# Moving the filter spectra behind the projections, with one third of the conditioning weights left ahead of them

## The reference, cut to what matters

```python
ada = silu(c) @ w_ada + b_ada                      # c: 1024, w_ada: 1024 x 6144
sh1, sc1, g1, sh2, sc2, g2 = split(ada, 6)         # six vectors of 1024
u = x * (1 + sc1) + sh1                            # needs the first third of ada
proj = u @ w_in                                    # Hyena, attention and gate parts
# Hyena branch: implicit filters, long convolution through spectra
h = sin(f1_freq * (feats @ f1_w + f1_b))           # 1024 x 64
h = sin(f2_freq * (h @ f2_w + f2_b))               # 1024 x 64, "hidden"
h = (h @ f3_w).reshape(1024, 2, 2, 512) * decay    # taps, forward and backward, 2 orders
K = rfft(concat([fwd, 0, reversed bwd]))           # spectra, independent of x and c
z = x1 * long_conv(v, K[:, 0]); z = x2 * long_conv(z, K[:, 1])
# attention branch, gates, output projection:
x = LN(alpha * x + (1 + g1) * mix)                 # needs the second third of ada
x = LN(alpha * x + (1 + g2) * peer(x * (1 + sc2) + sh2))   # PEER, 128 x 128 experts, top 16
```

## Time and profile before

| | us |
|---|---|
| median of three runs | 4256.4 |
| the execution that was profiled | 4264.03 |
| its span, first to last instruction | 4262.2 |
| setup, to the next stage's first transfer | 39.4 |
| spectra, to the next stage's first transfer | 200.5 |
| attention projections | 231.3 |
| attention and other projections, to the long convolution | 520.1 |

### The profile page before, as it was taken

The page is one execution under the profiler, slowest core; times in us unless marked ns, Lnnn a source line. Parts: engine busy times, 40 slices in busy tenths (PEclk is TensorE's granted clock), DMA queues, the critical chain, the costliest instruction groups (busy, mean ns, idle before and its releaser), DMA issues. The chain is left out here.

```text
span 4262.2 us, 57381 instructions
## 1 busy us (share of the span) xinstructions
PE 3770.9 (88%) x19170; PEld 3277.4 (77%) x19170; DVE 2565.5 (60%) x5465; ACT 1396.8 (33%) x2897; POOL 1153.5 (27%) x797
## 2 busy tenths in 40 slices
PE   6889899998879798999989889896888988898896
PEld 3579788886657687999988879896677777777775
DVE  5563133224544413999988778785766666666667
ACT  1110122221123211233278888796211111111111
POOL 1132121112322021333343333332323232323330
PEclk9789999998989899999999999898999999999998
DMA  4741212215543222333379999999867677777773
GB/s 176 285 148 40 81 65 81 76 61 217 197 147 124 79 80 90 130 131 132 119 249 329 305 313 322 294 333 304 293 241 238 238 240 244 236 244 246 242 256 136
DMA packets 502745, 826.90 MB, mean 194 GB/s; under 512 B 289175, under 2 KB 309911, under 8 KB 496440
## 3 DMA queue, kind: packets, MB, share of 16 engines
q1 hardware_dynamic: 111848, 370.03, 24.8%
q0 software_dynamic: 84096, 318.80, 21.2%
q10 hardware_dynamic: 306576, 135.28, 12.7%
HBM read 679.31 MB, written 144.70 MB: 193 GB/s over the span
## 5 line engine op out<-in xcount | busy, mean ns | idle before, releaser
L79 PE MATMUL va_fps<-va_vt_h,va_c_h 128*128 128x512 f32 x1536 | 631.1, 411 | 184.6 <-DVE va_vt_l L2204 176.0
L80 PE MATMUL va_fps<-va_vt_l,va_c_h 128*128 128x512 f32 x1536 | 621.9, 405 | 0.0
L81 PE MATMUL va_fps<-va_vt_h,va_c_l 128*128 128x512 f32 x1536 | 621.0, 404 | 0.0
L2082 POOL DMA_INDIRECT va_rows<-in_vtab,k_pick x256 | 377.3, 1474 | 850.4 <-DVE k_big L2228 748.0
L79 PEld LDWEIGHTS va_fps<-va_vt_h,va_c_h 128*128 128x128 f32 x1536 | 305.6, 199 | 262.9 <-issue 164.6
L1916 ACT ACTIVATE ga_first<-ga_first,ga_gs 128x128 f16<-128x128 f16 x1536 | 470.2, 398 | 85.0 <-DVE ga_first L1975 84.8
L79 PE MATMUL ga_aps<-k_u_h,k_ut_h 128*128 128x384 f32 x1152 | 404.6, 351 | 27.9 <-issue 20.8
L81 PE MATMUL ga_aps<-k_u_h,k_ut_l 128*128 128x384 f32 x1152 | 391.7, 340 | 8.0 <-issue 8.0
L80 PE MATMUL ga_aps<-k_u_l,k_ut_h 128*128 128x384 f32 x1152 | 391.3, 340 | 0.0
L2171 ACT ACTIVATE va_c_h<-va_c 128x768 fp32r<-128x768 f32 x128 | 108.1, 845 | 790.1 <-DVE va_c L2196 790.1
L80 PEld LDWEIGHTS va_fps<-va_vt_l,va_c_h 128*128 128x128 f32 x1536 | 305.7, 199 | 64.2
(11 more groups left out here) (295 smaller groups left out, 8078.0 us busy)
## 6 DMA issues: line engine op xcount, KB each, us to landing
k_ut<-in_utab SPq DMA_DIRECT2D x129, 512.0 KB, 5.5
va_vt<-in_vtab SPq DMA_DIRECT2D x128, 512.0 KB, 4.9
va_c<-scratch_ahead SPq DMA_DIRECT2D x128, 384.0 KB, 3.1
va_wt<-scratch_gates SPq DMA_DIRECT2D x128, 384.0 KB, 3.8
hy_tab<-in_tab POOLq DMA_DIRECT2D x64, 512.0 KB, 4.7
scratch_ahead<-ga_gelu_a ACTq DMA_DIRECT2D x72, 384.0 KB, 6.5
sp_wada<-in_w_ada SPq DMA_DIRECT2D x24, 1024.0 KB, 8.6
scratch_gates<-ga_wide ACTq DMA_DIRECT2D x32, 768.0 KB, 14.3
```

The source lines that it names most:

```text
L79: nc.tensor.matmul(out, w[0], x[0], start=first, stop=False)
L80: nc.tensor.matmul(out, w[0], x[1], start=False, stop=False)
L81: return nc.tensor.matmul(out, w[1], x[0], start=False, stop=last)
L2082: nc.gpsimd.indirect_dma_start(got[:, q % SLOTS_G, :], None, vrows, picked(K, q)).then_inc(got_in[q % SLOTS_G], 16)
```

## The change

- `stage_setup` no longer loads `f3_w` or forms `f3p`. It loads the first eight pieces of `w_ada` (8 MB) behind its small inputs, all at once into a buffer of their own, and PE sums them directly: 128 float32 products of one column each, with a piece of `w_ada` of 128x128 as the weights and `silu(c)` as the column (L175 in the new file). They stand behind the second sine layer on PE. DVE adds two partial sums. `silu` is computed first on ACT, and ACT stores the hidden layer to DRAM.
- `stage_spectra` runs behind `stage_mix`, ahead of `stage_hyena`. It loads `f3_w` and the hidden layer on SP's queue ahead of `decay`, forms `f3p`, and splits both into rounded halves (ACT the high part, DVE the rest). PE waits for both splits (`low_ok`). The taps are then three fp32r products in place of each float32 one.
- It keeps 16 pieces of `w_ada`, two steps to a unit. `finish(1)` stands behind unit 3, `finish(2)` behind unit 7, and `finish(0)` and the place behind unit 6 are gone.

```diff
+            for k in range(KT):
+                sp.dma_start(wada[:, k, :], T["w_ada"][0, k]).then_inc(ada_in[k // 4], 16)
             sp.wait_ge(loads, 16 * len(small))
             sp.sem_inc(ready, 1)
...
+            pe.wait_ge(act_s, 1)
+            for a in range(2):
+                pe.wait_ge(ada_in[a], 16 * 4)
+                for c in range(2 * KT):
+                    for k in range(4 * a, 4 * a + 4):
+                        last = nc.tensor.matmul(sums[:, a, c:c + 1], wada[:, k, c * P:(c + 1) * P], K["silu"][:, k:k + 1],
+                                                start=k % 4 == 0, stop=k % 4 == 3)
+                last.then_inc(ada_mm, 1)
...
+            for a in range(2):
+                dve.wait_ge(ada_mm, a + 1)
+                ch.link(nc.vector.tensor_tensor(both, sums[:, a, 0:2 * KT], both, ALU.add))
...
+            act.dma_start(S["hidden"], h2[:, :]).then_inc(kept, 16)
...
-        STEPS = 3 * KT
+        STEPS = 2 * KT
...
+            sp.dma_start(f3w, T["f3_w"].rearrange("p (a b) -> p a b", a=2)).then_inc(first_in, 16)
+            sp.dma_start(h2, S["hidden"]).then_inc(first_in, 16)
...
+            pe.wait_ge(low_ok, 2)
...
                     for j in range(2):
-                        last = nc.tensor.matmul(ps[:, 2 * (lt % 2) + j, :], K["h2"][:, lt % FT * 2 * P + lt // FT:(lt % FT + 1) * 2 * P:2],
-                                                K["f3p"][:, j, o, :], start=True, stop=True)
+                        last = product3(nc, ps[:, 2 * (lt % 2) + j, :], (h2_h[:, lt * P:(lt + 1) * P], h2_l[:, lt * P:(lt + 1) * P]),
+                                        (f3_h[:, j, o, :], f3_l[:, j, o, :]), True, True)
...
                     if (o, q) == (0, FT - 1):
-                        finish(0)
-                    if (o, q) == (1, FT - 2):
                         finish(1)
             finish(2)
...
+            act.wait_ge(first_in, 32)
+            nc.scalar.activation(h2_h[:, :], h2, ACT.Copy).then_inc(high_ok, 1)
+            act.wait_ge(f3_ok, 2)
+            nc.scalar.activation(f3_h[:, :, :, :].rearrange("p a b c -> p a (b c)"), f3p, ACT.Copy).then_inc(high_ok, 1)
...
-                    ada_step(3 * n)
                     for j in range(2):
-                        ada_step(3 * n + 1 + j)
+                        ada_step(2 * n + j)
...
-            stage_setup(nc, S, K, T)
-            stage_spectra(nc, S, K, T)
+        keep("silu", [P, KT])
+        stage_setup(nc, S, K, T)
...
             stage_qkv(nc, S, K, T)
             stage_mix(nc, S, K, T)
+        stage_spectra(nc, S, K, T)
```

More of the change, by code:

```diff
@@ L135, in stage_setup @@
         ps = ctx.enter_context(nc.psum_tensor("su_ps", [64, 2, HALF], F32))
+        sums = ctx.enter_context(nc.psum_tensor("su_sums", [P, 2, HALF], F32))
+        ada_in = [sem(f"ada_in{k}") for k in range(2)]
+        ada_mm, kept = sem("ada_mm"), sem("kept")
         loads, ready, layer, args_ok, hid = sem("loads"), sem("silu"), sem("layer"), sem("args"), sem("hidden")
@@ L144, in _ @@
                 (feats[:, :], T["feats"]), (f1w[:, :], T["f1_w"]), (f2w[:, :], T["f2_w"]),
-                (f3w[:, :, :].rearrange("p a b -> p (a b)"), T["f3_w"]), (fvec[:, :], T["fvec"]), (pos_i[:, :], T["positions"]),
+                (fvec[:, :], T["fvec"]), (pos_i[:, :], T["positions"]),
                 (inv[:, :], T["inv"].partition_broadcast(P)), (cc[:, :], T["c"]), (K["ident"][:, :], T["ident"]),
@@ L170, in _ @@
             dve.wait_ge(ready, 1)
-            for j, op in enumerate((ALU.add, ALU.subtract)):
-                ch.link(nc.vector.tensor_tensor(K["f3p"][:, j, :, :].rearrange("p a b -> p (a b)"), f3w[:, 0, :], f3w[:, 1, :], op))
             dve.wait_ge(layer, 1)
@@ L191, in _ @@
             ch.link(nc.vector.tensor_scalar(sc, sc, -2.0, 1.0, ALU.mult, ALU.add))
+            both = K["ada_col"][:, 0:2 * KT]
+            for a in range(2):
+                dve.wait_ge(ada_mm, a + 1)
+                ch.link(nc.vector.tensor_tensor(both, sums[:, a, 0:2 * KT], both, ALU.add))
         @block.scalar
         def _(act):
+            act.wait_ge(ready, 1)
+            nc.scalar.activation(K["silu"][:, :], cc[:, :], ACT.Silu).then_inc(act_s, 1)
             act.wait_ge(args_ok, 1)
@@ L219, in stage_spectra @@
         wada = sb("wada", [P, 2, 2 * D])
-        ada = sb("ada", [P, 6 * D])
+        ada = sb("ada", [P, 4 * D])
+        h2_h, h2_l = sb("h2_h", [64, SEQ], F32R), sb("h2_l", [64, SEQ], F32R)
+        f3_h, f3_l = sb("f3_h", [64, 2, 2, HW], F32R), sb("f3_l", [64, 2, 2, HW], F32R)
+        h2 = odd[0:64, :, :].rearrange("p a b -> p (a b)")
+        f3w, f3p = (spec[0:64, a, :, :].rearrange("p (a b) c -> p a (b c)", a=2) for a in range(2))
         ones = sb("ones", [P, P])
@@ L273, in finish @@
                     row = k % 3 == 2
-                    if third:
-                        pe.wait_ge(ada_out, 2 * third)
+                    if third > 1:
+                        pe.wait_ge(ada_out, 2)
                     if row:
                         for h in range(2):
-                            last = nc.tensor.matmul(ps[:, 2 * e + h, :], ones[:, :], ada[:, k * D + h * HALF:k * D + (h + 1) * HALF],
+                            last = nc.tensor.matmul(ps[:, 2 * e + h, :], ones[:, :], ada[:, (k - 2) * D + h * HALF:(k - 2) * D + (h + 1) * HALF],
                                                     start=True, stop=True)
@@ L349, in ada_step @@
             def ada_step(e):
-                third, k = divmod(e, KT)
-                part = ada[:, 2 * third * D:2 * (third + 1) * D]
+                half, k = divmod(e, KT)
+                part = ada[:, 2 * half * D:2 * (half + 1) * D]
                 dve.wait_ge(ada_in[e % 2], 16 * (e // 2 + 1))
@@ L362, in take @@
                     k = 2 * third + e
-                    dve.wait_ge(ada_mm, k + 1)
+                    dve.wait_ge(ada_mm, k - 1)
                     if k % 3 == 2:
@@ L371, in take @@
                         v.tensor_tensor(col, ps[:, 2 * e, 0:KT], col, ALU.add).then_inc(ada_out, 1)
+            dve.wait_ge(first_in, 32)
+            for j, op in enumerate((ALU.add, ALU.subtract)):
+                v.tensor_tensor(f3p[:, j, :], f3w[:, 0, :], f3w[:, 1, :], op).then_inc(f3_ok, 1)
             ch.link(v.memset(ones[:, :], 1.0))
+            dve.wait_ge(high_ok, 1)
+            v.tensor_tensor(h2_l[:, :], h2, h2_h[:, :].bitcast(F32), ALU.subtract).then_inc(low_ok, 1)
+            dve.wait_ge(high_ok, 2)
+            v.tensor_tensor(f3_l[:, :, :, :].rearrange("p a b c -> p a (b c)"), f3p,
+                            f3_h[:, :, :, :].rearrange("p a b c -> p a (b c)").bitcast(F32), ALU.subtract).then_inc(low_ok, 1)
             dve.wait_ge(decay_in, 32)
@@ L413, in _ @@
                     if (o, q) == (0, FT - 1):
-                        take(0)
-                    if (o, q) == (1, FT - 2):
                         take(1)
@@ L2303, in build @@
     dram("spec", (2, KT, P, 2, HW))
+    dram("hidden", (64, SEQ))
     dram("cm", (CM_TILES, P, SEQ))
@@ L2324, in build @@
         keep("ada_row", [P, 4, HALF])
-        early = ExitStack()
-        with early:
-            K["h2"] = early.enter_context(nc.sbuf_tensor("k_h2", [64, SEQ], F32))
-            K["f3p"] = early.enter_context(nc.sbuf_tensor("k_f3p", [64, 2, 2, HW], F32))
-            K["silu"] = early.enter_context(nc.sbuf_tensor("k_silu", [P, KT], F32))
-            stage_setup(nc, S, K, T)
-            stage_spectra(nc, S, K, T)
+        keep("silu", [P, KT])
+        stage_setup(nc, S, K, T)
         with (nc.sbuf_tensor("k_u1_h", [P, KT, SEQ], F32R) as u_h, nc.sbuf_tensor("k_u1_l", [P, KT, SEQ], F32R) as u_l,
@@ L2416, in layouts @@
     return {
-        "feats": feats.T, "f1_w": hy_f1_w[0], "f2_w": hy_f2_w[0], "f3_w": hy_f3_w[0],
+        "feats": feats[by_parity].T, "f1_w": hy_f1_w[0], "f2_w": hy_f2_w[0], "f3_w": hy_f3_w[0],
         "fvec": np.stack([hy_f1_b[0], hy_f1_freq[0], hy_f2_b[0], hy_f2_freq[0]], 1),
```

20 lines of the change are left out of this document (11 added, 9 removed).

## The result

| | before | after |
|---|---|---|
| median of four runs, us | 4260.4 (4254.12 to 4264.53) | 4285.9 (4282.18 to 4289.07) |
| the execution that was profiled | 4264.03 | 4289.07 |
| setup, to the next stage's first transfer | 39.4 | 82.2 |
| the two stages between setup and long convolution | 751.4 | 750.6 |
| spectra | 200.5 | 178.2 |

The kernel became slower: ratio 1.0061, 95% interval [1.0043, 1.0079], 25.5 us on the medians. The forecast was +14.0 us, with a range of 4250 to 4288 us (-6 to +32 on the median of three runs that it started from). The direction held; the time lies 2 us inside the range and outside the 4264 to 4277 of the forecast itself. The setup grew by 42.8 us (44.4 forecast); the spectra gave back 22.3 (30.4 forecast).

What follows compares the result with a forecast made beforehand. The setup was taken as bound by a PE, DVE and ACT chain, the spectra by `decay`, PE's taps, transfers and `finish`. Setup +44.4 and spectra -30.4 give +14.0 us on 4256.4, so 4270.4 us; range 4250 to 4288.

Steps and rivals of the forecast that it cites:

- Setup, +44.4: Setup: 256 one-column instructions at 0.213 us take 54.5 us on PE; the stage ends at 83.8 instead of 39.4.
- the two falls named there: Earlier trace: twice a run of one-column products began at the high clock and was at 0.50 before it ended.
- The rival of short loads: Setup: weight loads take 0.107 us, so it grows by only 17.3 us; sum -13.1, 4243 us; chance 0.07.
- that of held issues: Setup: SP is held up issuing transfers, so `ready` comes 8 us late; +22, 4278 us; chance 0.12.
- Start of the spectra, +4.0: Spectra up to `decay`: f3_w and the hidden layer ahead of it cost 4.2 us at 376 GB/s; bounds +2 and +8.
- Taps, -4.5 and -4.6: Taps of both orders: a tile takes PE 2.6 us instead of 3.4, a pair of tiles 5.85 instead of 6.8.
- Units, -9.0 and -8.5: Units to the ends of units 3 and 7: two steps and pieces instead of three; bounds 0 and -11.4 each.
- Around `finish`, -3.0: Spectra around `finish`: about 4 us of PE work, where DVE was late by a step before; bounds 0 and -4.
- End, -4.8: End of the spectra: the 4.95 us wait goes, and the last store becomes late next; 4.8 us shorter.
- Place, 0: Spectra's new position in the program: costs nothing, as the stage starts and ends at a barrier as before.
- the rival in which the traffic stays the bound: Spectra: tables keep 12.5 us, stores follow late, each long stretch of units gains only 3 us; +25.5, 4282 us; chance 0.19.
- a later stage changes by more than 3 us: Later stages: one of the signs by which the prediction said it would be wrong.

Runs made afterwards that it cites:

- kept_awake: The changed kernel with 98 wide bf16 products that nobody reads added to the setup; 17.0 us over the kernel before, ratio 1.0051, setup 85.9 us.
- first_alone: The changed kernel with POOL's two 2 MB tables issued only after f3_w and the hidden layer have landed; +21.6 us over the kernel before, ratio 1.0049.
- steps_first: The changed kernel with DVE's first conditioning step of a unit ahead of its wait for the store; +18.2 us over the kernel before, ratio 1.0043.
- spectra_back: The changed kernel with the spectra right behind the setup again, ahead of the projections; +23.8 us over the kernel before, ratio 1.0055.
- before_again: The kernel before, without any edit, profiled a second time; +0.4 us, ratio 1.0003.

## Why the prediction came out as it did

The mechanism was right, and two terms of the sum were mis-sized: the start of the spectra and the stretch around `finish`. Times in this list are first profile against first profile, both cut as in the windows of the changed kernel.

- *Setup, +44.4.* +42.8. The value was chosen between two that both stood in the earlier trace rows. The second of the two falls named there came behind 4.95 us without work, so only the first, at 136 us, is a fall under one-column products alone; kept_awake shows it cleanly. The stream took 54.77 us where 54.5 was worked out, and `ready` came 1.6 us earlier, with one load fewer ahead of it. The rival of short loads is refuted by the rows above and by kept_awake, that of held issues by `ready` at 10.21.
- *Start of the spectra, +4.0.* +10.5: this is the term that failed, 6.5 of the 8.1 us by which the spectra missed. I priced the new loads by their bytes at the 376 GB/s of the old start, and took their place at the queue's head for a near free way. In fact the 64-row transfers moved about half the bytes in the same time (199 GB/s with nothing beside them), and the tables, which POOL issued 0.5 us later on its own queue, moved beside them all the while: before the first multiplication 7.9 MB had moved, not 4.7 + 1.6, both tables whole and some 0.8 MB of `w_ada` among them. first_alone puts 5.8 us to the tables. The forecast's upper bound of +8 took the half rate alone; both causes together exceed it.
- *Taps, -4.5 and -4.6.* -5.3 and -4.0: a pair of tiles took 5.76 us (863.24, 869.00, 874.76) for 5.85 worked out. The prediction's own 23.7 - 19.6 us is 4.1, not 4.5.
- *Units, -9.0 and -8.5.* -7.8 and -9.2.
- *Around `finish`, -3.0.* 0.0, and +2.1 by the cut of the earlier trace rows (the taps then take some 6 us less in place of 4.0). The list of waits of before held the store's wait, 4.2 us once, and I didn't follow it: the steps and the pieces that `finish(1)` needs stand behind it in DVE's order, and once `w_ada` was no longer late by itself, it was. That chain is read from the trace; steps_first moved it by 1 us only, and the stretch takes 6.9 to 15.4 us from one execution to the next.
- *End, -4.8.* -6.5.
- *Place, 0.* 0, by spectra_back.

The total of 25.5 us is that of the rival in which the traffic stays the bound, and yet that rival is refuted: it gave each long stretch of units 3 us, and they gained 7.8 and 9.2. A total alone would have picked the wrong story; only the stretches tell them apart. All the same the traffic is what went wrong, ahead of the units, at the start of the stage. That the time lay inside the stated range is luck in part: the range reached up to 4288 for this rival's sake and for that of held issues, and neither happened.

By the sums ahead, 44.4 - 30.4 = +14.0 became 42.8 - 22.3 - 0.8 = +19.7 at the start of the long convolution in the first profiles, the 0.8 being the stages between. The sign "a later stage changes by more than 3 us" was met in the first profile of the changed kernel, by 6.7 us; before_again met it with no change at all, so it was set too fine.

Of the Trainium skill's rule (TensorE: Matmul & The Clock Gate, section LDWEIGHTS) that a load takes its columns over 1.2 GHz, 107 ns for 128, with no word on the state of the clock: the 256 loads took 213.6 ns each, and in kept_awake the first eight 115 and the rest 214. The figure is near that of the high clock; at the low one the measurement decides against it.

## What to carry to other kernels

Price a product of one column by its weight load, and a long stream of them at the low clock: the stream here didn't hold the high one, though a run of 15 did (1.75 us). A sum that VectorE does for 2.4 us a piece cost TensorE 6.8. When loads are put ahead of a stage's first work, price them by their rows and by what the other queues have under way, not by their place in their own queue; holding the big tables back by one wait made the start 5.8 us shorter. When a wait is taken away, look in the old list of waits for the short ones that stand in the same instruction stream: here one of them was late next. Where the list puts a long wait to `issue`, compare its end with the landing of what the instruction reads: here it was a transfer (922.76, the step at 922.84).

## What the runs showed of the hardware

- Transfers into 64 partitions: 199 GB/s with the transfer engines 95% busy, where 128-row transfers soon behind them moved 440 at 106% (first_alone).
- The weight load of a float32 product, 128 columns: 0.2136 us each over 256 at the low clock, 0.115 at the high one (kept_awake); there the high clock was lost 1.2 us after the narrow stream began, with wide products between its parts.
- The part from 2130 to 3030 us, in which POOL and DVE pass rows to each other, took between 10.1 us less and 6.7 us more in executions with the same instructions: a single profile can't settle anything under that size there.
